# Gate and up of a decoder layer: seven block products of 256 tokens in place of eight

## The chip, the cores and the metric

The kernel runs on 1 core of one Trainium2 chip. The metric is device time in microseconds (us), from one launch of the whole layer. Five engines of the core work side by side, each through its own instruction stream: TensorE (PE, with its weight loads as PEld), VectorE (DVE), ScalarE (ACT), GpSimd (POOL) and SyncE (SP), which here only issues DMAs. They are ordered by semaphores: an instruction waits until a counter has reached a value, and a finished one raises it.

## The reference

One decoder layer over 512 tokens of width 1024, in float32:

```
h = x
h = h + 0.5 * swiglu(rmsnorm(h), ffn1_w_gate, ffn1_w_up, ffn1_w_down)
u = rmsnorm(h);  proj = u @ w_in
merged = gate_pool * pool_branch(proj) + gate_attn * window_attention(proj)
h = h + merged @ w_out
h = h + 0.5 * swiglu(rmsnorm(h), ffn2_w_gate, ffn2_w_up, ffn2_w_down)

swiglu(x, w_gate, w_up, w_down) = (silu(x @ w_gate) * (x @ w_up)) @ w_down
```

The hidden width of both feed-forward networks (FFN) is 2816, 22 tiles of 128 (f-tiles). The change is in the products x @ w_gate and x @ w_up of both.

## The kernel before

Activations lie transposed: the 128 partitions hold channels, the free dimension holds the 512 tokens, and the 1024 channels are eight tiles (k-tiles). All weights come as one stream of 182 *units* of 512 KB, each 128 partitions by eight tiles of 128 columns. For gate and up, a unit is one f-tile: eight k-tiles of stationary weights. Units pass through four slots (`raw`, `high`, `low`).

Every product is made in three matmuls of a reduced float32 format (fp32r). A number is split into a high part, which that format holds, and a low part, what is left: `wh·xh + wh·xl + wl·xh` (`passes`, lines 320 to 327). So a unit is 24 matmuls of 128x128 by 512 columns. The high part of a unit is a copy on ScalarE (`refill`, line 604) that waits until TensorE has used the slot's last unit. The low part is a subtraction on GpSimd (`low_part`, line 858). SyncE loads the next unit into `raw` when the low part has been made (line 306).

`ffn_up` on TensorE (line 361) goes through the 22 f-tiles: gate unit, up unit, in PSUM banks 4 to 7 in turn. VectorE (`ffn_up`, line 961) scales both by `rinv`, the factor of the rmsnorm, which isn't ready until after the first products: `norm_factor` (line 952) is made while TensorE works on the first four units, and the fifth unit must wait until tile 0 has been scaled out of its bank. ScalarE makes the tanh (silu is made from it) and the high part of the hidden tile, VectorE its low part. Then `ffn_down` (line 390) multiplies the hidden tiles with 22 units of `w_down`. Queues of all engines are in order: an instruction that waits holds back all behind it on its engine.

Between the two FFNs come the projections, the pooling branch, the attention (lines 439 to 579) and the output projections. The change leaves their order as it is.

## Time and profile before

| | |
|---|---|
| Time, median of 3 runs | 1095.8 us (1095.75 to 1096.73) |
| Span of the profiled execution, first to last instruction | 1090.5 us |
| Time outside that span, against the median | 5.3 us |
| PE busy | 1073.4 us, 4872 matmuls |
| PEld busy | 874.1 us, 4872 |
| DVE busy | 507.5 us, 746 |
| ACT busy | 413.0 us, 623 |
| POOL busy | 475.4 us, 208 |
| HBM read | 98.17 MB, 92 GB/s over the span |

The page of the profile lists no time of the profiled execution beside its span; its own time is taken as the median, 5.3 us over the span. Busy shares are averages over the whole span. PE's matmuls overlap in the records (each is listed some 0.39 us long, but they start every 0.23 us), so its pace is read from starts. In the first part of FFN1 (gate and up, 34.6 to 265 us) PE was busy in 230.3 of 230.4 us, DVE in 120.2, ACT in 84.6 and POOL in 108.1.

### The profile page before, as it was taken

What the parts mean: (1) busy time and instruction counts of PE and PEld (TensorE: products, weight loads), DVE (VectorE), ACT (ScalarE), POOL (GpSimd) and SP (SyncE); (2) the same over time, 40 slices, a digit from 0 to 9 for tenths busy, and PEclk for the clock granted to TensorE, in tenths of its full rate; (3) what the DMA queues carried; (4) which work ended last, traced back from release to release, by engine and by line L of the source; (5) the groups of instructions that cost most, each with busy time, mean ns of one, the idle gap of its engine ahead of it and who ended that gap; (6) DMA issues with size and microseconds to landing.
All of it is one profiled execution on the core that took longest, in us unless ns stands there. A gap on an engine that the chain in (4) does not pass through costs nothing.

```text
span 1090.5 us, 13935 instructions
## 1 busy us (share of the span) xinstructions
PE 1073.4 (98%) x4872; PEld 874.1 (80%) x4872; DVE 507.5 (47%) x746; ACT 413.0 (38%) x623; POOL 475.4 (44%) x208
## 2 busy tenths in 40 slices
PE   7999999999999999999999999999999999999998
PEld 5788888888888887887777788888888888888887
DVE  6854454543030386326766656676454545430101
ACT  6334333332131324247676643343333333421110
POOL 1553444444444424345545444444444444444440
PEclk9999999999999999999999999999999999999999
DMA  6333333323223222221111122323222322333331
GB/s 229 113 115 96 96 96 96 96 87 107 96 81 112 78 87 97 78 93 63 58 58 58 59 78 97 97 78 105 93 95 92 97 95 96 96 97 96 97 97 38
DMA packets 28684, 100.67 MB, mean 92 GB/s; under 512 B 3312, under 2 KB 3312, under 8 KB 28656
## 3 DMA queue, kind: packets, MB, share of 16 engines
q1 hardware_dynamic: 28512, 100.02, 28.2%
q8 instruction: 19, 0.31, 0.1%
q10 hardware_dynamic: 144, 0.26, 0.1%
q14 instruction: 9, 0.07, 0.0%
HBM read 98.17 MB, written 2.10 MB: 92 GB/s over the span
## 4 chain that ended last, share of the span: by engine, by line
PE 91%; DVE 6%; issue 1%; ACT 1%; DMA 1%; SPq 0%; DVEq 0%; ACTq 0%
PE psum L325 29%; PE psum L327 29%; PE psum L326 28%; DVE window_sums L1060 1%; PE psum L513 1%; PE psum L528 1%; PE psum L541 1%; PE psum L542 1%; PE psum L543 1%; DVE rinv L957 1%; PE psum L434 1%; DMA h<-x_dram 1%; DVE probs L1136 1%; DVE probsT_low L1172 0%; DVE score_max L1141 0%
## 5 line engine op out<-in xcount | busy, mean ns | idle before, releaser
L861 POOL TENSOR_TENSOR w_low<-w_raw,w_high 128x1024 fp32r<-128x1024 f32 x180 | 439.1, 2441 | 521.7 <-ACT w_high L610 521.7
L325 PE MATMUL psum<-u_high,w_high 128*128 128x512 f32 x944 | 375.5, 398 | 9.2 <-DVE w_low L1019 7.5
L327 PE MATMUL psum<-u_high,w_low 128*128 128x512 f32 x944 | 371.7, 394 | 0.0
L326 PE MATMUL psum<-u_low,w_high 128*128 128x512 f32 x944 | 369.3, 391 | 0.0
L610 ACT ACTIVATE w_high<-w_raw 128x1024 fp32r<-128x1024 f32 x180 | 190.3, 1058 | 333.0 <-PE psum L327 332.8
L325 PEld LDWEIGHTS psum<-u_high,w_high 128*128 128x128 f32 x944 | 177.8, 188 | 49.8 <-DVE w_low L1019 7.5
L326 PEld LDWEIGHTS psum<-u_low,w_high 128*128 128x128 f32 x944 | 177.9, 188 | 39.8 <-issue 1.0
L327 PEld LDWEIGHTS psum<-u_high,w_low 128*128 128x128 f32 x944 | 177.7, 188 | 38.8
L327 PE MATMUL psum<-hid_high,w_low 128*128 (+1 forms) x352 | 138.3, 393 | 0.0
L325 PE MATMUL psum<-hid_high,w_high 128*128 (+1 forms) x352 | 137.6, 391 | 0.0
L326 PE MATMUL psum<-hid_low,w_high 128*128 (+1 forms) x352 | 137.3, 390 | 0.0
L978 DVE TENSOR_TENSOR up<-up,gate 128x512 f32<-128x512 f32 x44 | 118.1, 2685 | 1.5
L943 DVE SCALAR_TENSOR_TENSOR h<-psum,h 128x512 f32<-128x512 f32 x24 | 16.6, 692 | 216.4 <-PE psum L327 216.3
L971 DVE TENSOR_TENSOR up<-psum,rinv 128x512 f32<-128x512 f32 x44 | 30.4, 691 | 179.0 <-PE psum L327 179.0
L645 ACT ACTIVATE hid_high<-up 128x512 f32 x44 | 27.8, 632 | 136.8 <-DVE up L978 136.8
L326 PEld LDWEIGHTS psum<-hid_low,w_high 128*128 128x128 f32 x352 | 66.1, 188 | 15.1
L327 PEld LDWEIGHTS psum<-hid_high,w_low 128*128 128x128 f32 x352 | 66.1, 188 | 14.3
L325 PEld LDWEIGHTS psum<-hid_high,w_high 128*128 128x128 f32 x352 | 66.1, 188 | 14.0
L883 POOL TENSOR_TENSOR probs<-probs,inv_denominator 128x1024 f32<-128x1024 f32 x16 | 30.3, 1896 | 71.6 <-DVE inv_denominator L1154 71.6
L980 DVE TENSOR_TENSOR hid_low<-up,hid_high 128x512 f32 x44 | 32.9, 747 | 40.2 <-ACT hid_high L645 40.2
L777 ACT ACTIVATE probs<-probs,neg_max,rq_now 128x256 f32<-128x256 f32 x64 | 37.6, 595 | 2.5 <-DVE sink_minus_max L1147 2.1
L932 DVE SCALAR_TENSOR_TENSOR u_low<-h,params,u_high 128x512 fp32r<-128x512 f32 x24 | 30.7, 1295 | 14.1 <-ACT u_high L622 13.9
(146 smaller groups left out, 932.3 us busy)
## 6 DMA issues: line engine op xcount, KB each, us to landing
w_raw<-weights_dram SPq DMA_DIRECT2D x181, 512.0 KB, 3.3
out_dram<-h SPq DMA_DIRECT2D x8, 256.0 KB, 3.2
h<-x_dram SPq DMA_DIRECT2D x3, 512.0 KB, 6.7
h<-x_dram SPq DMA_DIRECT2D x2, 256.0 KB, 4.2
w_raw<-weights_dram SPq DMA_DIRECT2D x2, 256.0 KB, 4.4
consts<-consts_dram SPq DMA_DIRECT2D x1, 352.0 KB, 9.1
poolw_raw<-poolw_dram ACTq DMA_DIRECT2D x1, 256.0 KB, 3.5
params<-params_dram SPq DMA_DIRECT2D x1, 31.0 KB, 1.8
```

Source lines behind the costliest of these rows:

```text
L325: pe.matmul(o, wh, xh, start=start, stop=False)
L326: pe.matmul(o, wh, xl, start=False, stop=False)
L327: return pe.matmul(o, wl, xh, start=False, stop=stop)
L610: act.activation(high[:, s, :], raw[:, s, :], ACT.Copy).then_inc(high_done, 1)
L645: act.activation(F["hid_h"][:, bass.ds(f, 1), :], F["up"][:, k:k + 1, :], ACT.Copy).then_inc(F["hidden_high"], 1)
L777: act.activation(prob[:, j % 2, a, :], prob[:, j % 2, a, :], ACT.Exp, bias=nmax[:, j % 2, a:a + 1], scale=rqn[:, 4 * j + a:4 * j + a + 1], ...
L861: pool.tensor_tensor(low[:, s, :], raw[:, s, :], high[:, s, :], ALU.subtract).then_inc(low_done, 1)
L883: pool.tensor_tensor(p, p, rden[:, j % 2, :].unsqueeze(2).to_broadcast([P, 4, 2 * BLK]), ALU.mult).then_inc(probs_ready, 1)
L932: dve.scalar_tensor_tensor(out=tile(lo, c), in0=tile(h, c), scalar=at(gains[n], c), in1=tile(hi, c), op0=ALU.mult, op1=ALU.subtract).then_ ...
L971: dve.tensor_tensor(v, psum[:, 5 + 2 * k, :], rinv[:, :], ALU.mult).then_inc(F["up_scaled"], 1)
L978: dve.tensor_tensor(v, v, g, ALU.mult).then_inc(F["hidden"], 1)
L980: dve.tensor_tensor(tile(F["hid_l"], f), v, tile(F["hid_h"], f), ALU.subtract).then_inc(F["hidden_low"], 1)
```

## The change

The products of gate and up run over *pairs* of f-tiles in all but the first tiles of each FFN: 6 plain f-tiles and 8 pairs in FFN1, 4 plain and 9 pairs in FFN2 (`PLAIN`, `PAIRS`). A pair's weights are 2 x 2 blocks (two f-tiles by two halves of the k-tiles), the normed activations 2 x 2 blocks as well (halves of the k-tiles by halves of the tokens, 256 each). Four blocks times four blocks would be eight block products; the kernel makes seven out of sums of blocks (the scheme of Strassen and Winograd). A block product is 4 k-tiles x 3 passes = 12 matmuls of 256 columns; gate and up together are 14 products a pair, at positions 0 to 13 in this order: a11 gate, a12 gate, a11 up, a12 up, s2 gate, s1 gate, s2 up, s1 up, s3 gate, s4 gate, s3 up, s4 up, a22 gate, a22 up.

- Weights of a pair, for gate and for up: `a1` (two blocks) and `s31` (two blocks) are loaded, 512 KB each, and `a22` a second time, 256 KB. GpSimd makes two sums in place in `s31` (`sum_blocks`), VectorE two more, `s2` and `s4` (`weight_sums`). ScalarE makes the high parts of all, VectorE the low parts of `a1`, `s2`, `s31`, GpSimd those of `s4` and `a22` (`late_lows`). Low parts overwrite the full values.
- Activations, once an FFN: `scale_blocks` makes the normed input (now times `rinv` beforehand, 8 instructions of 512 elements a partition), `sum_blocks` on VectorE four sums of 1024, ScalarE seven high parts of 1024, `moving_lows` seven low parts of 1024.
- Results of a pair: since the products are shared among outputs, ScalarE copies six partial results of 256 tokens out of PSUM (`copy_part`) and VectorE adds six others to them (`add_part`). `second_tile` finishes the pair's second f-tile (four instructions of 256 tokens) at the start of the next pair in VectorE's stream.
- High and low parts of the hidden tiles are made late, in the last pair and beside the down products, since their memory is that of the activation blocks.
- In the plain and down units the low part overwrites `raw`, so SyncE loads a unit when TensorE has used the slot (`load_used`) and no longer when its low part is made. All loops of the FFNs are written out. Every tensor has a fixed address.

The core of the diff; comments and blank lines are left out.

```diff
+PLAIN = (6, 4)
+PAIRS = tuple((FT - p) // 2 for p in PLAIN)
+STEPS = 14
...
+            def load_used(u):
+                sp.wait_ge(unit_used, u - SLOTS + 1)
+                load(u)
+            def pairs(n):
+                for i in range(PAIRS[n]):
+                    if i + 1 < PAIRS[n]:
+                        sp.wait_ge(product, done(n, i, 1))
+                        load_a1(n, i + 1, 0, gate_w)
+                        sp.wait_ge(product, done(n, i, 3))
+                        load_a1(n, i + 1, 1, up_w)
+                    if i + 2 < PAIRS[n]:
+                        sp.wait_ge(product, done(n, i, 8))
+                        load_s31(n, i + 2, 0, gate_w)
+                        sp.wait_ge(product, done(n, i, 10))
+                        load_s31(n, i + 2, 1, up_w)
+                    if i + 1 < PAIRS[n]:
+                        sp.wait_ge(product, done(n, i, 12))
+                        load_a22(n, i + 1, 0, gate_w)
+                        sp.wait_ge(product, done(n, i, 13))
+                        load_a22(n, i + 1, 1, up_w)
...
+            def multiply(bank, wh, wl, xh, xl, fresh):
+                o = psum[:, bank, 0:HT]
+                for c in range(HALF):
+                    w = slice(c * P, (c + 1) * P)
+                    pe.matmul(o, wh[:, w], xh[:, c, :], start=fresh and c == 0, stop=False, skip_group_check=not fresh)
+                    pe.matmul(o, wh[:, w], xl[:, c, :], start=False, stop=False, skip_group_check=not fresh)
+                    mm = pe.matmul(o, wl[:, w], xh[:, c, :], start=False, stop=c == HALF - 1,
+                                   skip_group_check=not fresh)
+                mm.then_inc(product, 1)
...
+            def pair(n, i, F):
...
+                def a11(k, w):
+                    pe.wait_ge(w["low"], 3 * g + 1)
+                    if i >= 2:
+                        pe.wait_ge(pair_hidden if k else pair_silu, 3 * g - 3)
+                    else:
+                        pe.wait_ge(F["up_scaled" if k else "gate_scaled"], PLAIN[n] - 1)
+                    moving(1)
+                    multiply(x + k, w["a_h"][:, one], w["a_l"][:, one], ub_h[:, B11], ub_l[:, B11], True)
...
+                def s2(k, w):
+                    pe.wait_ge(w["low"], 3 * g + 2)
+                    pe.wait_ge(part_copied, 6 * g + 1 + k)
+                    moving(3)
+                    multiply(x + k, w["s2_h"], w["s2_l"], ts_h[:, NT2], ts_l[:, NT2], False)
...
+                def a22(k, w):
+                    pe.wait_ge(w["late"], 2 * g + 2)
+                    pe.wait_ge(part_summed, 6 * g + 3 + 2 * k)
+                    moving(7)
+                    multiply(x + k, w["a22_h"], w["a22_l"], ts_h[:, T4], ts_l[:, T4], False)
+                for k, w in enumerate((gate_w, up_w)):
+                    a11(k, w)
+                    a12(k, w)
+                for k, w in enumerate((gate_w, up_w)):
+                    s2(k, w)
+                    s1(k, w)
+                for k, w in enumerate((gate_w, up_w)):
+                    s3(k, w)
+                    s4(k, w)
+                a22(0, gate_w)
+                a22(1, up_w)
...
+            def plain(n, base, F):
+                p = PLAIN[n]
+                g = first_pair(n)
+                for f in range(p - 4):
+                    plain_tile(n, base, f, F)
+                for b in (B11, B21, B22):
+                    block_high(n, b)
+                plain_tile(n, base, p - 4, F)
+                for t, count in ((NT2, 2), (NT1, 2), (T3, 3), (T4, 4)):
+                    sum_high(n, t, count)
+                plain_tile(n, base, p - 3, F)
+                high_a1(g, gate_w)
+                high_s2(g, gate_w)
+                high_s31(g, gate_w)
+                plain_tile(n, base, p - 2, F)
+                high_a1(g, up_w)
+                high_s2(g, up_w)
+                high_s31(g, up_w)
+                plain_tile(n, base, p - 1, F)
+            def pair(n, i, base, F):
+                g = first_pair(n) + i
...
+                more = i + 1 < PAIRS[n]
...
+                act.wait_ge(product, done(n, i, 0))
+                if i:
+                    act.wait_ge(pair_hidden, 3 * g - 2)
+                else:
+                    act.wait_ge(F["hidden"], PLAIN[n])
+                copy_part(gate_t[:, 0, left], x)
+                if i:
+                    act.wait_ge(product, done(n, i - 1, 12))
+                high_late(g, gate_w)
+                act.wait_ge(product, done(n, i, 2))
+                copy_part(up[:, 0, left], x + 1)
+                if i:
+                    act.wait_ge(product, done(n, i - 1, 13))
+                else:
+                    act.wait_ge(unit_used, base + 2 * PLAIN[n])
+                high_late(g, up_w)
+                act.wait_ge(product, done(n, i, 4))
+                copy_part(gate_t[:, 0, right], x)
+                act.wait_ge(product, done(n, i, 5))
+                if i:
+                    act.wait_ge(pair_hidden, 3 * g)
+                copy_part(gate_t[:, 1, right], 6)
+                if more:
+                    high_a1(g + 1, gate_w)
+                act.wait_ge(product, done(n, i, 6))
+                copy_part(up[:, 0, right], x + 1)
+                act.wait_ge(product, done(n, i, 7))
+                copy_part(up[:, 1, right], 7)
+                if more:
+                    high_a1(g + 1, up_w)
+                    high_s2(g + 1, gate_w)
+                    act.wait_ge(product, done(n, i, 8))
+                    high_s31(g + 1, gate_w)
+                else:
+                    refill(base + 2 * PLAIN[n], 0, U_DN1 // SLOTS + 1 if not n else U_DN2 // SLOTS + 1, first=True)
+                    for f in range(4):
+                        hidden_high(n, f, F)
+                act.wait_ge(part_summed, 6 * g + 4)
+                if i:
+                    act.wait_ge(pair_silu, 3 * g)
+                act.activation(th[:, 0, :], gate_t[:, 0, :], ACT.Tanh, scale=0.5).then_inc(pair_tanh, 1)
+                if more:
+                    high_s2(g + 1, up_w)
+                    act.wait_ge(product, done(n, i, 10))
+                    high_s31(g + 1, up_w)
+                else:
+                    hidden_high(n, 4, F)
+                    hidden_high(n, 5, F)
+                act.activation(th[:, 1, right], gate_t[:, 1, right], ACT.Tanh, scale=-0.5).then_inc(pair_tanh, 1)
+                act.wait_ge(product, done(n, i, 12))
+                act.activation(th[:, 1, left], psum[:, x, left], ACT.Tanh, scale=-0.5).then_inc(pair_tanh, 1)
...
+            def sum_blocks(g, w):
+                s31, one, two = w["s31"][g % 2], slice(0, UNIT // 2), slice(UNIT // 2, UNIT)
+                pool.wait_ge(w["s31_landed"][g % 2], 16 * (g // 2 + 1))
+                pool.tensor_tensor(s31[:, two], s31[:, two], s31[:, one], ALU.add)
+                pool.wait_ge(w["a_landed"], 16 * (g + 1))
+                pool.tensor_tensor(s31[:, one], s31[:, one], w["a"][:, one], ALU.add).then_inc(w["s31_summed"][g % 2], 1)
+            def late_lows(g, w):
+                pool.wait_ge(w["high"], 5 * g + 4)
+                pool.tensor_tensor(w["s4_l"][g % 2][:, :], w["s4"][g % 2][:, :], w["s4_h"][:, :],
+                                   ALU.subtract).then_inc(w["late"], 1)
+                pool.wait_ge(w["high"], 5 * g + 5)
+                pool.tensor_tensor(w["a22_l"][:, :], w["a22"][:, :], w["a22_h"][:, :],
+                                   ALU.subtract).then_inc(w["late"], 1)
+            def ffn(n, base, first):
+                for u in range(base + first, base + 2 * PLAIN[n]):
+                    low_part(u, u % SLOTS, raw_low)
+                    if u == base + 4:
+                        sum_blocks(first_pair(n), gate_w)
+                sum_blocks(first_pair(n), up_w)
+                for i in range(PAIRS[n]):
+                    g = first_pair(n) + i
+                    late_lows(g, gate_w)
+                    if i + 1 < PAIRS[n]:
+                        sum_blocks(g + 1, gate_w)
+                    late_lows(g, up_w)
+                    if i + 1 < PAIRS[n]:
+                        sum_blocks(g + 1, up_w)
+                b = base + 2 * PLAIN[n]
+                for u in range(b, b + 2 * DOWN):
+                    low_part(u, u % SLOTS, raw_low)
...
+            def scale_blocks(n):
+                for c in range(DT):
+                    kh, kt = c // HALF, c % HALF
+                    dve.scalar_tensor_tensor(
+                        out=ub[:, 2 - 2 * kh:4 - 2 * kh, kt, :], in0=h[:, c, :].rearrange("p (a t) -> p a t", a=2),
+                        scalar=at(gains[2 * n], c), in1=rinv[:, :].rearrange("p (a t) -> p a t", a=2),
+                        op0=ALU.mult, op1=ALU.mult).then_inc(u_scaled, 1)
+            def sum_blocks(n):
+                dve.wait_ge(u_scaled, DT * (n + 1))
+                dve.tensor_tensor(ts[:, NT1], ub[:, B11], ub[:, B12], ALU.subtract).then_inc(ts_summed, 1)
...
+            def moving_lows(n):
+                for lo, full, hi, count in (
+                        (ub_l[:, B11], ub[:, B11], ub_h[:, B11], 1), (ub_l[:, B21], ub[:, B21], ub_h[:, B21], 2),
...
+            def weight_sums(g, w):
+                dve.wait_ge(w["a_landed"], 16 * (g + 1))
+                dve.wait_ge(w["s31_summed"][g % 2], g // 2 + 1)
+                s1 = w["s31"][g % 2][:, UNIT // 2:UNIT]
+                dve.tensor_tensor(w["s2"][:, :], s1, w["a"][:, 0:UNIT // 2], ALU.add).then_inc(w["summed"], 1)
+                dve.wait_ge(w["summed"], 2 * g + 1)
+                dve.tensor_tensor(w["s4"][g % 2][:, :], w["s2"][:, :], w["a"][:, UNIT // 2:UNIT], ALU.add
+                                  ).then_inc(w["summed"], 1)
...
+            def plain(n, base, F):
+                p = PLAIN[n]
+                g = first_pair(n)
+                for f in range(p - 4):
+                    plain_tile(n, base, f, F)
+                scale_blocks(n)
+                plain_tile(n, base, p - 4, F)
+                sum_blocks(n)
+                plain_tile(n, base, p - 3, F)
+                moving_lows(n)
+                weight_sums(g, gate_w)
+                plain_tile(n, base, p - 2, F)
+                low_a1(g, gate_w)
+                low_s2(g, gate_w)
+                low_s31(g, gate_w)
+                dve.wait_ge(unit_used, base + 2 * p - 1)
+                weight_sums(g, up_w)
+                low_a1(g, up_w)
+                plain_tile(n, base, p - 1, F)
+                low_s2(g, up_w)
+                low_s31(g, up_w)
...
+            def pair(n, i, F):
+                g = first_pair(n) + i
+                x = 4 * ((i + PAIRS[n]) % 2)
+                f = PLAIN[n] + 2 * i
+                more = i + 1 < PAIRS[n]
+                def add_part(to, bank, pos, copied):
+                    dve.wait_ge(product, done(n, i, pos))
+                    dve.wait_ge(part_copied, 6 * g + copied)
+                    dve.tensor_tensor(to, psum[:, bank, left], to, ALU.add).then_inc(part_summed, 1)
+                if i:
+                    second_tile(n, i - 1)
+                add_part(gate_t[:, 0, left], 2, 1, 1)
+                add_part(up[:, 0, left], 3, 3, 2)
+                if more:
+                    dve.wait_ge(product, done(n, i, 4))
+                    weight_sums(g + 1, gate_w)
+                    low_a1(g + 1, gate_w)
+                    dve.wait_ge(product, done(n, i, 6))
+                    weight_sums(g + 1, up_w)
+                    low_a1(g + 1, up_w)
+                    low_s2(g + 1, gate_w)
+                add_part(gate_t[:, 1, right], x, 8, 4)
+                if more:
+                    low_s31(g + 1, gate_w)
+                else:
+                    hidden_low(0, F)
+                    hidden_low(1, F)
+                add_part(gate_t[:, 0, right], 6, 9, 3)
+                add_part(up[:, 1, right], x + 1, 10, 6)
+                add_part(up[:, 0, right], 7, 11, 5)
+                if more:
+                    low_s2(g + 1, up_w)
+                    low_s31(g + 1, up_w)
+                dve.wait_ge(pair_tanh, 3 * g + 1)
+                dve.scalar_tensor_tensor(out=gate_t[:, 0, :], in0=th[:, 0, :], scalar=1.0, in1=gate_t[:, 0, :],
+                                         op0=ALU.add, op1=ALU.mult).then_inc(pair_silu, 1)
+                dve.wait_ge(pair_silu, 3 * g + 1)
+                dve.wait_ge(part_summed, 6 * g + 6)
+                dve.tensor_tensor(hid[:, f, :], gate_t[:, 0, :], up[:, 0, :], ALU.mult).then_inc(pair_hidden, 1)
```

## Rows read from the trace of the kernel before

**Rows 1.** The page: span and busy us of each engine.

```profile
span 1090.5 us, 13935 instructions
...
PE 1073.4 (98%) x4872; PEld 874.1 (80%) x4872; DVE 507.5 (47%) x746; ACT 413.0 (38%) x623; POOL 475.4 (44%) x208
```

**Rows 2.** PE in order of time inside FFN1: start, duration, line; 24 matmuls of 512 columns apart.

```profile
100.01 0.39 PE L325 MATMUL psum<-u_high,w_high 128*128 128x512 f32 x1
...
105.50 0.39 PE L325 MATMUL psum<-u_high,w_high 128*128 128x512 f32 x1
```

**Rows 3.** The same view in the attention: 256 columns, two row halves at once, four steps apart.

```profile
490.68 0.28 PE L513 MATMUL psum<-k_block_low,q_block_high 64*128 64x256 f32 x2
...
491.16 0.28 PE L513 MATMUL psum<-k_block_high,q_block_low 64*128 64x256 f32 x2
```

**Rows 4.** The same view: eight matmuls of two columns, each with a weight load.

```profile
465.18 0.95 PE L434 MATMUL psum<-consts,q_squares 128*128 128x2 f32 x8
```

**Rows 5.** DVE and POOL in order of time in FFN1.

```profile
102.04 2.42 POOL L861 TENSOR_TENSOR w_low<-w_raw,w_high 128x1024 fp32r<-128x1024 f32 x1 [3.09 <-ACT w_high L610]
...
102.22 2.78 DVE L978 TENSOR_TENSOR up<-up,gate 128x512 f32<-128x512 f32 x1
```

**Rows 6.** DVE and POOL in order of time, both with several instructions queued.

```profile
410.39 5.23 POOL L861 TENSOR_TENSOR w_low<-w_raw,w_high 128x1024 fp32r<-128x1024 f32 x2 [4.82 <-ACT w_high L610]
...
410.85 2.50 DVE L1060 TENSOR_TENSOR window_sums<-pool_in 128x512 f32<-128x512 f32 x1
413.38 4.23 DVE L1060 TENSOR_TENSOR window_sums<-window_sums 128x512 f32<-128x512 f32 x3
```

**Rows 7.** Groups by line: busy us, mean ns of one, idle before, releaser.

```profile
L610 ACT ACTIVATE w_high<-w_raw 128x1024 fp32r<-128x1024 f32 x180 | 190.3, 1058 | 333.0 <-PE psum L327 332.8
...
L799 ACT ACTIVATE attn_high<-psum 64x256 fp32r<-64x256 f32 x8 | 3.0, 373 | 3.2 <-PE psum L543 3.1
...
L877 POOL TENSOR_TENSOR v_block_low<-v_tokens,v_block_high 128x256 fp32r<-128x256 f32 x4 | 2.9, 729 | 0.0
```

**Rows 8.** DVE in order of time, and the POOL instruction beside its last two.

```profile
519.97 1.28 DVE L1114 SCALAR_TENSOR_TENSOR q_block_low<-q,params,q_block_high 128x1024 fp32r<-128x1024 f32 x1
...
420.06 0.68 DVE L1047 TENSOR_TENSOR k_raw<-psum,rinv 128x512 f32<-128x512 f32 x1
420.67 0.68 DVE L1047 TENSOR_TENSOR v_raw<-psum,rinv 128x512 f32<-128x512 f32 x1
...
420.45 2.36 POOL L861 TENSOR_TENSOR w_low<-w_raw,w_high 128x1024 fp32r<-128x1024 f32 x1 [4.84 <-ACT w_high L610]
```

**Rows 9.** Start of FFN1: POOL, PE and DVE in order of time.

```profile
28.71 2.42 POOL L861 TENSOR_TENSOR w_low<-w_raw,w_high 128x1024 fp32r<-128x1024 f32 x1 [2.73 <-ACT w_high L610]
...
34.66 0.49 PE L325 MATMUL psum<-u_high,w_high 128*128 128x512 f32 x1 [1.54 <-DVE gate L968]
...
78.92 0.69 DVE L971 TENSOR_TENSOR up<-psum,rinv 128x512 f32<-128x512 f32 x1 [4.67 <-PE psum L327]
```

**Rows 10.** Start of FFN2: DVE and ACT in order of time.

```profile
735.08 1.99 DVE L948 TENSOR_TENSOR sum_of_squares<-rinv 128x512 f32<-128x512 f32 x1
...
738.30 0.69 DVE L959 TENSOR_TENSOR rinv<-rinv,sum_of_squares 128x512 f32<-128x512 f32 x1
...
746.80 0.69 DVE L971 TENSOR_TENSOR up<-psum,rinv 128x512 f32<-128x512 f32 x1 [1.34 <-PE psum L327]
...
768.77 0.69 DVE L971 TENSOR_TENSOR up<-psum,rinv 128x512 f32<-128x512 f32 x1 [4.68 <-PE psum L327]
...
732.98 1.06 ACT L610 ACTIVATE w_high<-w_raw 128x1024 fp32r<-128x1024 f32 x1
```

**Rows 11.** PE in order of time in the first matmuls of the kernel.

```profile
8.50 0.63 PE L327 MATMUL psum<-u_high,w_low 128*128 128x512 f32 x1
8.93 0.63 PE L325 MATMUL psum<-u_high,w_high 128*128 128x512 f32 x1
```

**Rows 12.** DMA issues of the page: KB each, median us from issue to landing.

```profile
w_raw<-weights_dram SPq DMA_DIRECT2D x181, 512.0 KB, 3.3
```

614 lines of the change are left out of this document (413 added, 201 removed).

## The prediction

> **What bounds the kernel now.** I read the page first. The reader is to see that TensorE is busy in 98% of the span [rows 1]; so the end moves with its work and its waits. In order of time its starts inside FFN1 are evenly spaced: 24 matmuls of 512 columns, one unit, take 105.50 - 100.01 = 5.49 us, 0.229 us each [rows 2]. The other engines have room, but VectorE and GpSimd don't use theirs independently. At 102.04 GpSimd starts a subtraction of 2.42 us, at 102.22 VectorE a product of two tensors in SBUF, which ends at 105.00: GpSimd's end plus the 0.55 that it needs itself [rows 5]. With both queues full they take turns: GpSimd's two take 5.23 instead of 4.8 (one VectorE instruction lies between them), and VectorE's take 2.5 instead of 0.6 each time they meet one [rows 6]. So every instruction of VectorE with two SBUF inputs and every one of GpSimd share one resource, and its time adds up. An instruction with one input in PSUM isn't held: two of them start 0.61 apart, 0.68 long, over a GpSimd subtraction that runs from 420.45 [rows 8].
>
> **What is removed: matmul time.** Before, two f-tiles are four units, 4 x 5.49 = 21.96 us. A pair is 14 products x 12 = 168 matmuls of 256 columns. The trace has no such matmul over 128 rows. The nearest are those of the attention: 256 columns in two row halves start every (491.16 - 490.68) / 4 = 0.120 us [rows 3]. Bounds: half of a 512-column one, 0.1145 [rows 2]; and with a weight load that doesn't hide well, 0.127: eight weight loads with two columns each behind them need about 0.11 apiece (0.95 less some 0.2 of the last one's length, over seven) [rows 4], and 0.229 - 0.1145 leaves 0.015 a matmul for what doesn't shrink. I take 0.120: a product 1.44 us, a pair 20.2 us (19.2 to 21.3). If nothing else waited, 17 pairs would give back 17 x 1.8 = 31 us (11 to 47).
> The Trainium skill (TensorE: Matmul & The Clock Gate, "Wait — 56ns, not 53.3ns?") has 2.4 GHz matmuls start every N/2.4 + 2.5 ns, 109 ns at 256 columns; the trace disagrees at 512 (229 against 216). By it a pair would be 18.3 us; it would only matter where TensorE sets the pace.
>
> **What is added, by duration.** VectorE with two SBUF inputs: 512 elements hold it 0.60 (start to start 0.61 [rows 8]), 1024 about 1.15 (1.28 long, next one earlier [rows 8]), 256 about 0.35. GpSimd: 1024 elements 2.42 [rows 5], 256 0.73 [rows 7], so 512 by the line between them 1.29, 1.24 back to back (bounds 1.2 and 1.3). ScalarE: 1024 1.06, 256 0.37 [rows 7], 512 about 0.6. A handover from TensorE costs 0.2, others 0.1 (102.04 + 2.42 to VectorE's next).
>
> **A pair in the steady state.** The shared resource: GpSimd 8 x 1.24 = 9.9; VectorE weight sums 4 x 0.6, lows of a1 and s31 4 x 1.15, of s2 2 x 0.6, silu and product of the first tile 1.2, of the second 0.7, in all 10.1. Together 20.0 us of a 20.2 us pair, before any wait for order. In order, with M the time in the pair at which VectorE has finished the previous pair's first tile (the copy of the first product into that buffer waits for it):
> - ScalarE copies and makes the high part of s4: M + 1.15. GpSimd makes its two gate lows and the two gate sums of the next pair, 4 x 1.24: Z = M + 6.1. The a1 load waits for position 1 (3.1) and lands 3.3 later [rows 12], 6.4: not late.
> - From Z VectorE's first weight sum may start, but GpSimd's next is queued and goes first, as in [rows 6]. They alternate: four of GpSimd (4.8), two weight sums and the a1 low of VectorE (2.3): Z + 7.1. Only now are the up sums there: two weight sums, two lows, 2.95, and the add of position 8, 0.35: Z + 10.4. TensorE's position 12 waits for this add. At Z = 9 that is 19.4, against 17.3 at TensorE's pace: a stall of 2.1 us.
> - Behind it stand the s31 low and two adds; the second releases position 13 at Z + 12.35, which ends at P = Z + 13.8.
> - ScalarE's tanh waits for an add (Z + 11.9), and two highs behind it hold back VectorE's last low to Z + 14.3; with silu and product VectorE is through at Z + 16.7 = P + 2.9. So M = 2.9, Z = 9.0 and P = 22.8 us.
> The bounds are 20.3 (turns fall out well, TensorE sets the pace) and 23.8 (some more handovers). I take 22.8, since each step is a row or lies in order: 0.8 a pair *slower* than four units. The last pair of each FFN has no weight sums and runs at TensorE's 20.2. 13 steady pairs: +10.9 (range -21 to +24); 2 last: -3.6.
>
> **Start of the pairs in FFN2.** Baseline: VectorE sees unit 3 end at 746.80 and unit 7, the last plain one, at 768.77 [rows 10]. `rinv` comes at 737.7, 1.3 earlier than now (738.30 + 0.69, less the 1.3 that the instruction at 735.08 waited for GpSimd): no GpSimd instruction falls on it, since the high of unit 4, now made at 732.98 [rows 10], stands in ScalarE's queue behind three highs that wait for `scale_blocks`.
> - scale_blocks 8 x 0.6: 742.8. Three highs and unit 4's: 746.9; its low 749.4. TensorE wanted it at 746.6: stall 2.8.
> - Then GpSimd makes the two gate sums before unit 5's low, taking turns with the silu of tile 0 and VectorE's sums: 756.3, stall 1.5. Unit 6's high stands behind the highs of the sums, which wait for VectorE: low at 764.9, stall 3.0. Unit 7 ends at 775.9, 7.3 late.
> - VectorE: tile 1 until 768.3; seven moving lows 7.9 with two GpSimd sums between, 778.6; weight sums 779.8; tile 2 with tanh 782.9; the gate a1 low 784.1. Position 0 waits for it: 8.2 more. Position 2 waits for the up a1 low, 788.2: 1.15 more. The pair is 17.0 late.
> - In this pair GpSimd's lows start at 792.0 (tile 3's product, then copy and high), 6.4 in the pair where the steady state has 4.1; the same chain gives a22 4.9 late, a pair of 25.5: 3.5 over four units.
> **In FFN1** two tiles stand before `scale_blocks`, but GpSimd's two gate sums now follow unit 4's low (28.71 to 31.1 [rows 9]) and fall on the steps of `rinv`: 2.1 later, and TensorE already waits there, at 34.66 after 1.54 of idle [rows 9]. Then unit 10's low 1.9 late, and by the same list VectorE's gate a1 low at 90.9 instead of 78.7 (unit 11's end [rows 9]), the up one 4.1 later: 13.7 late. First pair +3.5.
> Bound of both from below: without turns VectorE's list in FFN2 (27 us of its own from 737.7, some 6 of waits for tanh) ends at 771, 2 late; half of each chain seems the least, 20 together; from above 48. I take 17.0 + 13.7 + 7.0 = 37.7.
>
> **What stays.** The down products: loads of units now wait for TensorE (3.3 + 1.06 + 2.42 = 6.8 and handovers [rows 5, 7, 12], needed 16.5 later), hidden lows 0.6 each against two a unit of 5.49: hidden. 256 KB more per matrix and pair, some 130 GB/s: hidden. Attention and projections: unchanged. Unrolled code removes table loads of ScalarE, which had idle time: 0.
>
> **Sum.** 37.7 + 10.9 - 3.6 = +45 us on a profiled execution of 1090.5 span [rows 1] and 5.3 outside, which is the median 1095.8: 1141 us.
>
> **Rivals.**
> 1. *TensorE sets the pace in the pairs* (turns fall better than in my list: VectorE's ops get in ahead of GpSimd's queued ones). P = 20.3 in 13 pairs: -21.6 instead of +10.9: 1095.8 + 37.7 - 21.6 - 3.6 = 1108. For it: 20.0 us of shared work fit in 20.2. Against: [rows 6] shows the queued GpSimd instruction goes on first.
> 2. *The other side, faster:* the turns exist but the block work before the pairs is covered. Its place is the stretch from `rinv` to position 0, its price 20 us in place of 37.7; it decides for faster once the pairs run at 20.3 too and the two starts cost less than 25: 1095.8 + 20 - 21.6 - 3.6 = 1091. For it: by VectorE's own durations the list is only 2 us late. Against: every meeting in [rows 5, 6].
> 3. *The clock falls in the stalls.* The kernel's first matmuls start every 0.43 us, 1.2 GHz, for 4.6 us [rows 11], after idle time. The stalls of 8 us ahead of position 0 may bring this back, 2.3 us each by these rows; most of it lies under VectorE's lateness. 1141 to 1146. The Trainium skill (the same page, "HAM oscillation") says that gaps of TensorE re-throttle it; no stretch inside this trace shows it.
> 4. *The 256-column matmuls don't hide their weight load* (0.106 + 0.11 = 0.22): a pair of 36 us: 1095.8 + 17 x 14 = over 1330. Against: [rows 3] have a load in every step.
>
> **Chances.** Forecast 0.55 (own range 1125 to 1158), rival 1 and what lies between 0.22, rival 2 0.12, clock 0.06, loads 0.02, no visible change (gains and starts cancel) 0.03. Range 1100 to 1158, which leaves out rival 2 and the loads. A measurement of this kernel tells 0.2% (2.2 us) from no change. Faster 0.12, within 0.03, slower 0.85.
>
> **What would show it.** Start to start of the 256-column matmuls 0.120; a pair's period on TensorE 22.8 with idle ahead of positions 12 and 13, put down to VectorE's adds; idle before position 0 of 8 us in each FFN, put down to the a1 low; unit 4 of FFN2 waiting for its low; GpSimd's and VectorE's SBUF instructions nowhere overlapping. Wrong if TensorE shows no idle in the pairs, or if position 0 starts within 3 us of the last plain unit.

## The result, and the profile after

| | before | after |
|---|---|---|
| Time, median of 4 runs each | 1095.9 us (1095.75 to 1096.73) | 1144.9 us (1142.59 to 1146.99) |
| Ratio | | 1.0446 [1.0430, 1.0463] |
| Span of the profiled execution | 1090.5 us | 1142.9 us |

The change makes the kernel 49 us slower; 1141 was forecast. The page of the changed kernel answers to [rows 1]: TensorE is busy for less time, in a longer span. The row of its clock has eights where the pairs begin in FFN1, and in the plain tiles and the first pair of FFN2, and the chain that ended last runs 18% on VectorE and 14% on GpSimd.

```profile
span 1142.9 us, 15754 instructions
...
PE 1064.4 (93%) x6096; PEld 927.1 (81%) x6096; DVE 699.8 (61%) x1022; ACT 482.1 (42%) x838; POOL 517.5 (45%) x276
...
PEclk9998999999999999999999999998889999999999
...
PE 57%; DVE 18%; POOL 14%; issue 5%; ACT 4%; DMA 2%; DVEq 0%; SPq 0%; ACTq 0%
```

The two profiled executions lie 52.4 us apart, the medians 49.0. The profile of the kernel before is of an execution at full clock (1.000). Of its 48 executions beside the later runs, 8 have that clock: they take 1091.9 to 1093.0 us, and each span is 1.8 us shorter than its time. So that profile stands for about 1092.3 us and not for the median, and the time outside the span is 1.8 us in both kernels (1144.8 for a span of 1142.9). The 5.3 us of the table ahead of the prediction are these 1.8 and 3.5 of clock.

The waits of PE in the changed kernel, longest sum first (us in all, times, longest). Line 1505 is `add_part`, the wait of 13 steady pairs ahead of position 12. Line 1432 is the low part of a1 ahead of position 0. The "issue" waits are those ahead of position 12 in the two first pairs (5.13 and 4.78). They are waits for the same add: in FFN1 position 12 starts at 115.03, and VectorE's add for it ran from 114.51 to 114.93. L1241 is the low part of a plain unit.

```profile
PE psum L529 <- DVE gate L1505: 25.9, 13, 2.3
PE psum L529 <- DVE gate_a_low L1432: 13.6, 2, 7.6
PE psum L529 <- issue: 9.9, 2, 5.1
PE psum L476 <- POOL w_low_in_place L1241: 7.2, 3, 3.0
PE psum L476 <- DVE w_low_in_place L1584: 6.8, 1, 6.8
```

**Where the 52.4 us of span went.** All are differences of starts on PE. Position 0 comes at 90.52 in FFN1, where unit 12 came at 78.72: +11.8. In FFN2 it comes 59.62 after the first product of the FFN, for 44.82: +14.8. The two first pairs take 28.95 and 29.36 for 21.97, four units: +14.4. The 13 steady pairs take 23.0 on the mean: +13.4. The last two take 20.4 and 20.2: -3.4. The stretch from the end of gate and up in FFN1 to FFN2 is 2.6 longer: 4.3 more at the norm and the first projections, less what the down and output products save. The last down products are 1.2 shorter. The sum is 52.4.

Start of FFN1's pairs on PE in the changed kernel (start, duration, idle before and releaser in brackets). The reader is to see the idle before position 0, then matmuls 0.21 apart until 94.53 and 0.12 after it, and the same again from 115.03, which is position 12 of the first pair.

```profile
82.56 0.39 PE L478 MATMUL psum<-ffn_u_high,w_low_in_place 128*128 128x512 f32 x1
90.52 0.58 PE L529 MATMUL psum<-u_blocks_high,gate_a_high 128*128 128x256 f32 x1 [7.58 <-DVE gate_a_low L1432]
...
94.32 0.41 PE L531 MATMUL psum<-u_blocks_high,gate_a_low 128*128 128x256 f32 x1
94.53 0.32 PE L529 MATMUL psum<-u_blocks_high,gate_a_high 128*128 128x256 f32 x1
94.81 0.28 PE L531 MATMUL psum<-u_blocks_high,gate_a_low 128*128 128x256 f32 x1
...
115.03 0.51 PE L529 MATMUL psum<-moving_sums_high,gate_a_high 128*128 128x256 f32 x1 [5.13 <-issue]
...
118.32 0.36 PE L529 MATMUL psum<-moving_sums_high,up_a_high 128*128 128x256 f32 x1
118.52 0.28 PE L530 MATMUL psum<-moving_sums_low,up_a_high 128*128 128x256 f32 x1
```

The same by stretches (start and end, length, busy us and count of PE, PEld, DVE, ACT and POOL, granted clock, DMA share, GB/s): the first pair of FFN1, the six after it, the first pair of FFN2. The granted clock is 0.87 and 0.80 in the first pairs and 0.98 in the six between.

```profile
90.52:119.47 28.95, 23.82 (x169) 23.63 (x169) 21.95 (x27) 12.52 (x22) 12.45 (x8) 0.87 0.24 77
119.47:257.98 138.51, 126.10 (x1010) 124.19 (x1009) 99.91 (x133) 62.49 (x114) 71.73 (x48) 0.98 0.33 108
...
809.84:839.20 29.36, 24.58 (x168) 24.40 (x169) 22.37 (x28) 12.52 (x22) 12.45 (x8) 0.80 0.24 81
```

**A steady pair**, the fourth of FFN1, position 0 at 164.43. GpSimd, VectorE and the wait of PE that ends last. GpSimd's first four run from 168.26 to 173.29. Then VectorE's two sums and a low, 0.69 and 1.22 long when alone, take 1.67, 1.67 and 2.14, because GpSimd's next instruction goes first each time. VectorE is free for the up sums at 180.32, and the add that TensorE waits for starts at 183.59, after two lows.

```profile
168.26 1.30 POOL L1253 TENSOR_TENSOR gate_s_low<-gate_s,gate_s_high 128x512 fp32r<-128x512 f32 x1 [11.08 <-ACT gate_s_high L906]
...
173.26 1.29 POOL L1253 TENSOR_TENSOR up_s_low<-up_s,up_s_high 128x512 fp32r<-128x512 f32 x1
174.51 1.74 POOL L1256 TENSOR_TENSOR up_a_low<-up_a,up_a_high 128x512 fp32r<-128x512 f32 x1
...
177.91 2.28 POOL L1249 TENSOR_TENSOR up_s<-up_s,up_a 128x512 f32<-128x512 f32 x1
...
173.43 1.67 DVE L1424 TENSOR_TENSOR gate_s<-gate_s,gate_a 128x512 f32<-128x512 f32 x1 [2.61 <-POOL gate_s L1249]
...
176.90 2.14 DVE L1432 TENSOR_TENSOR gate_a_low<-gate_a,gate_a_high 128x1024 fp32r<-128x1024 f32 x1
180.32 0.69 DVE L1424 TENSOR_TENSOR up_s<-up_s,up_a 128x512 f32<-128x512 f32 x1 [1.28 <-POOL up_s L1249]
...
183.59 0.42 DVE L1505 TENSOR_TENSOR gate<-psum,gate 128x256 f32<-128x256 f32 x1
...
184.15 0.36 PE L529 MATMUL psum<-moving_sums_high,gate_a_high 128*128 128x256 f32 x1 [2.28 <-DVE gate L1505]
```

### The profile page after: what moved, and what is told of

Its sections match the earlier page's. It is cut to its first block, busy times and chain, and to the rows that moved or that the text cites. A ratio compares the mean times of both kernels' runs of the same rounds, so it can differ in the third digit from the quotient of the medians.

```text
span 1142.9 us, 15754 instructions
## 1 busy us (share of the span) xinstructions
PE 1064.4 (93%) x6096; PEld 927.1 (81%) x6096; DVE 699.8 (61%) x1022; ACT 482.1 (42%) x838; POOL 517.5 (45%) x276
## 4 chain that ended last, share of the span: by engine, by line
PE 57%; DVE 18%; POOL 14%; issue 5%; ACT 4%; DMA 2%; DVEq 0%; SPq 0%; ACTq 0%
PE psum L476 14%; PE psum L478 13%; PE psum L477 13%; PE psum L529 4%; PE psum L530 4%; PE psum L531 4%; POOL up_s L1249 3%; POOL up_s L1247 2%; POOL up_a_low L1256 2%; POOL gate_s L1249 2%; POOL up_s_low L1253 2%; POOL gate_s_low L1253 1%; DVE window_sums L1625 1%; POOL gate_a_low L1256 1%; POOL gate_s L1247 1%
## 5 line engine op out<-in xcount | busy, mean ns | idle before, releaser
L1241 POOL TENSOR_TENSOR w_low_in_place<-w_raw,w_high 128x1024 fp32r<-128x1024 f32 x62 | 153.8, 2485 | 210.8 <-ACT w_high L848 210.7
L848 ACT ACTIVATE w_high<-w_raw 128x1024 fp32r<-128x1024 f32 x112 | 117.9, 1054 | 191.9 <-DMA w_raw<-weights_dram 150.2
L1241 POOL TENSOR_TENSOR w_low<-w_raw,w_high 128x1024 fp32r<-128x1024 f32 x50 | 122.8, 2456 | 117.6 <-ACT w_high L848 117.6
L477 PE MATMUL psum<-hidden_low,w_high 128*128 128x512 f32 x352 | 137.0, 389 | 0.0
L476 PE MATMUL psum<-hidden_high,w_high 128*128 128x512 f32 x352 | 137.0, 389 | 0.0
L478 PE MATMUL psum<-hidden_high,w_low_in_place 128*128 128x512 f32 x352 | 137.0, 389 | 0.0
L476 PE MATMUL psum<-u_high,w_high 128*128 128x512 f32 x240 | 98.9, 412 | 0.4 <-DVE u_low L1341 0.3
L477 PE MATMUL psum<-u_low,w_high 128*128 128x512 f32 x240 | 94.1, 392 | 0.0
L478 PE MATMUL psum<-u_high,w_low 128*128 128x512 f32 x240 | 94.0, 392 | 0.0
L476 PE MATMUL psum<-ffn_u_high,w_high 128*128 128x512 f32 x160 | 66.7, 417 | 17.3 <-POOL w_low_in_place L1241 7.2
L477 PEld LDWEIGHTS psum<-hidden_low,w_high 128*128 128x128 f32 x352 | 66.1, 188 | 13.7
```

The source lines that it names most:

```text
L476: pe.matmul(o, wh, xh, start=start, stop=False)
L477: pe.matmul(o, wh, xl, start=False, stop=False)
L478: return pe.matmul(o, wl, xh, start=False, stop=stop)
L848: act.activation(high[:, s, :], raw[:, s, :], ACT.Copy).then_inc(high_done, 1)
L1241: pool.tensor_tensor(wlow[:, s, :], raw[:, s, :], high[:, s, :], ALU.subtract).then_inc(low_done, 1)
```

## The experiments

Theory 1 is the prediction's: GpSimd and VectorE take turns, and the order of the queues makes the turns late for TensorE. Experiments e1 to e5 and e8 test it, and its rival in each is named in the expectation. Experiments e6, e7, e9 and e10 are about something found in the traces and not foreseen.

### e1: GpSimd's pair work without reading SBUF

Each of the eight instructions becomes two fills; each fill waits for the one before it. The sums s3 and s1 and the low parts of s4 and a22 are thus not computed.

```diff
 def sum_blocks(g, w):
-    pool.tensor_tensor(s31[:, two], s31[:, two], s31[:, one], ALU.add)
+    fill(s31[:, two])
+    fill(s31[:, two])
...
```

> Each of the eight GpSimd instructions of a pair (two sums in s31, the lows of s4 and a22, for gate and up) is replaced by two fills with zero of the same 512 elements, with the same waits; so the weight sums and those lows are not computed. GpSimd then reads nothing from SBUF but keeps its place in the order. Theory 1 (GpSimd and VectorE take turns at SBUF): VectorE's two-input instructions are no longer held, means fall to 0.69 us (512 elements) and 1.22 (1024) in the pairs, and a steady pair falls from 23.0 to 20.3-20.8 us; the run to 1080-1105 us. Theory 2 (the pair is bound by the order of the queues and by GpSimd's own chain, not by turns): if the two fills last as long as one sum (some 1.2-1.3 us), the steady pair stays within 0.5 of 23.0. The trace shows how long a fill is; if it is far shorter, the run tells only an upper bound.

Measured: 1089.0 us, span 1087.0, in a single run, so there is no interval. VectorE's two groups of the gate sums and the low of a1, first as the changed kernel has them, then as e1 has them (count, busy us, mean ns):

```profile
L1432 DVE TENSOR_TENSOR gate_a_low<-gate_a,gate_a_high 128x1024 fp32r<-128x1024 f32 x17 | 34.5, 2029 | 1.6
L1424 DVE TENSOR_TENSOR gate_s<-gate_s,gate_a 128x512 f32<-128x512 f32 x17 | 26.4, 1554 | 38.9 <-POOL gate_s L1249 38.9
```

```profile
L1442 DVE TENSOR_TENSOR gate_a_low<-gate_a,gate_a_high 128x1024 fp32r<-128x1024 f32 x17 | 20.8, 1224 | 9.8 <-ACT gate_a_high L895 9.6
L1434 DVE TENSOR_TENSOR gate_s<-gate_s,gate_a 128x512 f32<-128x512 f32 x17 | 11.8, 691 | 27.9 <-POOL gate_s L1259 24.7 <-PE psum L532 3.2
```

Every pair but the first of each FFN takes 20.16 us, 14 x 1.44, with no wait. GpSimd still has work in every place (two fills take about 1.1 us, one instruction before 1.3), and VectorE now runs beside it. The shorter fills alone don't explain it: they bring VectorE's first sum from 9.0 to 7.9 us in the pair, and the add that TensorE waits for now ends 1.4 us before it is needed. So without the turns the written order is not late. The first pairs are 24.0, so the turns account for 5 of the 7 us there. Theory 1 is shown for the steady pair. The Trainium skill (SBUF — State Buffer, "SBUF: two separate sides") says that a VectorE instruction with two SBUF inputs locks out GpSimd only where that one reads SBUF; the rows agree on both halves, 1554 against 691 ns.

### e2: the late high parts ahead of the copy on ScalarE

```diff
+if i: act.wait_ge(product, done(n, i - 1, 12))
+high_late(g, gate_w)
 act.wait_ge(product, done(n, i, 0))
 ...
 copy_part(gate_t[:, 0, left], x)
-if i: act.wait_ge(product, done(n, i - 1, 12))
-high_late(g, gate_w)
```

> One move on ScalarE in every pair: the high parts of gate's s4 and a22 stand ahead of the copy of the first product, which waits for VectorE's last product of the pair before. Theory 1 (the cycle VectorE's end M -> copy -> highs -> GpSimd -> weight sums sets the steady pair): GpSimd starts with the pair, the first weight sum comes at 7.9 instead of 9.0 in the pair (then the landing of a1 is next), a steady pair 21.7 us instead of 23.0, a first pair 24-25 instead of 29, the whole 1145 - 13 x 1.3 - 2 x 4.5 = 1119 us (1110-1127). Theory 2 (the shared SBUF work alone sets the pair, order is indifferent): within 3 us of 1145.

Measured: 1131.9 us (1130.68 to 1133.12), ratio 1.0335 [1.0309, 1.0360]. The steady pairs fall from 23.0 to 22.1, where 21.7 was expected: GpSimd starts earlier, and the turns then come earlier. The first pairs stay at 28.2 and 29.2, where 24 to 25 was expected. Position 12 still starts at 23.9 in them, for 24.5. ScalarE comes to these instructions only after the tanh of the last plain tile, which waits for VectorE. GpSimd then starts 6.2 us into FFN1's first pair for 8.1, but its first four instructions take 6.9 for 5.6, in turns with VectorE's last plain product and the up lows. So VectorE's first sum comes at 13.3 for 13.9. The total of 1119 was missed by 13, most of it there. Theory 2 (within 3 us of 1145) is refuted.

### e3: VectorE's adds in the order in which TensorE wants them

On top of e2. The add of position 8 goes ahead of the up sums, that of 10 ahead of the low of s31, that of 11 behind it.

```diff
     low_a1(g + 1, gate_w)
-    dve.wait_ge(product, done(n, i, 6))
-    weight_sums(g + 1, up_w); low_a1(g + 1, up_w); low_s2(g + 1, gate_w)
 add_part(gate_t[:, 1, right], x, 8, 4)
 if more:
-    low_s31(g + 1, gate_w)
+    weight_sums(g + 1, up_w); low_a1(g + 1, up_w)
 add_part(gate_t[:, 0, right], 6, 9, 3)
 add_part(up[:, 1, right], x + 1, 10, 6)
+if more:
+    low_s2(g + 1, gate_w); low_s31(g + 1, gate_w)
 add_part(up[:, 0, right], 7, 11, 5)
```

> As the run with the highs first, and VectorE takes the add of position 8 before the up weight sums and those of 9 and 10 before the lows of gate's s2 and s31. Theory 1: positions 12 and 13 no longer wait, TensorE's stalls in the steady pairs go to under 0.5 us, a steady pair 20.3-21.0 us, the whole 1102 us (1095-1112). Theory 2 (20 us of turns in a pair of 20.2 can't be packed): the steady pair stays at 21.5 or more, the stall moves from position 12 to positions 0-4 of the next pair or to the a1 lows, and the whole stays within 4 us of the run with the highs first.

Measured: 1106.7 us (1106.46 to 1107.82), ratio 1.0107 [1.0083, 1.0130]. Position 12 now follows position 11 without a wait; what is left of the waits of PE is this (view as above):

```profile
PE psum L529 <- DVE gate_a_low L1430: 15.1, 2, 7.6
...
PE psum L529 <- issue: 5.4, 4, 1.8
PE psum L529 <- ACT gate L911: 2.8, 11, 0.3
```

The steady pairs take 20.4 to 20.8, and 21.6 the one behind FFN2's first. The 0.4 over TensorE's own 20.16 is position 4's wait for a copy on ScalarE. The same work, still in turns, is 2.4 us a pair cheaper in another order than as changed. So the loss takes both: the turns (e1) and an add that TensorE waits for queued late behind them.

### e4: the high parts of the plain units ahead of those of the blocks

Alone, on the changed kernel. ScalarE makes the highs of units 4 to 7 (in FFN1 8 to 11) two at a time ahead of the three and of the four block highs.

```diff
+units_of(base, p - 4)
 for b in (B11, B21, B22):
     block_high(n, b)
-plain_tile(n, base, p - 4, F)
+plain_tile(n, base, p - 4, F, False)
+units_of(base, p - 3)
 ...
```

> Only the start of the pairs: ScalarE makes the high parts of the next plain units before those of the activation blocks and of their sums. Theory 1 (VectorE's list of block work, in turns with GpSimd, sets position 0): the stalls of units 4 to 7 of FFN2 and of unit 10 of FFN1 go (9 and 2 us), but position 0 comes at most 2 us earlier in each FFN; the whole 1145 - 0 to 4 us. Theory 2 (the order of the highs on ScalarE sets the start): position 0 comes 7-9 us earlier in FFN2 and 2 in FFN1; the whole about 1135 us.

Measured: 1138.0 us (1136.78 to 1140.27), ratio 1.0386 [1.0361, 1.0410]. Position 0 comes 1.6 earlier in FFN1 and 2.4 earlier in FFN2: the stalls of the plain units of FFN2 stay, now as waits for VectorE (2.46 and 4.15). These are 4.0 of the 4.5 us between the two profiled spans; the medians are 7 apart, and the other 2.4 are in no trace. In FFN2 positions 0 and 1 now take 4.39 for 5.15, since the clock falls later there, and yet position 12 comes 24.49 after position 0 in both kernels; the section on the prediction comes back to it. Theory 1 allowed 2 us of start in each FFN and 4 in all, theory 2 7 to 9 in FFN2: the first has the place right, but the time came out past its bound.

### e5: the three orders together

> The changed kernel with all three orders of the earlier experiments at once: the four unit highs ahead of the block highs and ScalarE's late block highs ahead of its other late work, and VectorE's additions for the sums made early in the pair. Theory 1 (the steady pair is set by the turns of GpSimd and VectorE, and the first pair by ScalarE's order and the clock) adds the effects: the pair-level orders gave 1106.7, and the unit order took 2.4 us off the second start, left pair 8's products at nearly full clock and was worth 7 us on the changed kernel; some of that is the same clock time that the other orders give back, so 1100 us, between 1097 and 1104. Rival (the first pair is late for its sums only, which the unit order does not touch): 1104 to 1107.

Measured: 1103.8 us (1102.93 to 1105.31), ratio 1.0079 [1.0060, 1.0098]. This is the upper end of what was expected and the lower end of the rival's, so the total does not decide between them. The starts do: position 0 comes at 87.77 for e3's 88.62, and 57.03 after the start of FFN2 for 59.66, while the first pairs stay at 25.5 and 25.2 for 26.1 and 25.2.

### e8: six plain f-tiles in FFN2 as well

```diff
-PLAIN = (6, 4)
+PLAIN = (6, 6)
```

On e5: one pair less in FFN2, two plain f-tiles more. The expectation describes this edit wrongly (six for eight, and one pair more).

> The experiment with all orders (e5), with six plain units for eight ahead of the pairs and so one more pair in each FFN, if its number of tiles allows it. Theory 1: with a steady pair of 20.5 us for two units of 10.9 (21.9 for two positions of the before) each further pair for two plain units takes 1.4 us off, and the pair that comes first is put where the norm of the second half still runs: 2 to 4 us less than e5, 1096 us (1092 to 1102). Rival (the pair-level lists need the plain units as cover: their blocks are not ready when the pair begins, and TensorE waits for them): 1102 to 1112, slower than e5.

Measured: 1096.6 us (1094.84 to 1097.34), ratio 1.0008 [0.9997, 1.0019]; 7.2 less than e5. The number that was expected came, by the opposite of the reason given for it. The pair's 20.6 us become four units of 5.44, 21.8, so 1.1 is lost there. But position 0 now comes 70.39 after the start of FFN2, and without the four further units that is 48.6 for 57.03. The stalls of the plain units of FFN2 are gone, and a gap of 4.1 ahead of its position 0 is left:

```profile
PE psum L529 <- DVE gate_a_low L1436: 4.1, 1, 4.1
PE psum L529 <- issue: 2.9, 2, 1.8
```

So what FFN2 lacked was plain work for TensorE beside the block work. More than six isn't possible in this layout, since the seventh hidden tile lies on the normed input that plain tiles still read; it wasn't tried.

### e6, e7, e9, e10: where the operands lie

The changed kernel's 512-column matmuls start every 0.2268 us and not every 0.2289, also in the down products. There 24 of them, one unit, take 5.44 where [rows 2] have 5.49:

```profile
300.13 0.39 PE L476 MATMUL psum<-hidden_high,w_high 128*128 128x512 f32 x1
...
305.57 0.39 PE L476 MATMUL psum<-hidden_high,w_high 128*128 128x512 f32 x1
```

Every tensor has another address there. The four experiments leave the kernel before as it is and only add unused memory: 64 bytes ahead of the weight buffers (e6), the same and 64 behind them (e7), 192 behind them (e9), 128 behind them (e10).

```diff
 low = sb("w_low", [P, SLOTS, UNIT], F32R)
+pad_b = sb("pad_b", [P, 48])
 consts = sb("consts", [P, CONSTS])
```

> The kernel before with 64 bytes of unused memory ahead of its weight buffers, nothing else: every buffer moves up 64 bytes, so that weight tiles begin at 64 and activation tiles at 0 modulo 128 bytes in a partition, where in the kernel before it is the other way round. The 512-column product runs at 0.2289 us a matmul in the kernel before and 0.2268 in the changed one, also in the attention part that the change leaves alone. Theory A (the moving operand's address sets it; in the changed kernel both kinds of tile begin at 64): the rhs here is at the other phase than in both, so the pitch is anything between; if the stationary side or the sum of both counts, it stays 0.2289 and the time 1095.8; if weights at 64 are what is fast, 0.2268 and 1087, from some 4,370 matmuls by 2.1 ns. Theory B (the placement has no part in it, the mix of the program has): 0.2289 and 1095.8.

> The kernel before with 64 unused bytes ahead of the weight buffers and 64 more ahead of the constants, so that weight and activation tiles both begin at 64 modulo 128 bytes, as in the changed kernel; the instructions are the same. Theory A (the placement of operands sets the pitch of 512-column matmuls): pitch 0.2268 for 0.2289, 4,370 matmuls by 2.1 ns, 9 us less: 1087 us (1085 to 1089), less than both kernels. Theory B (placement has no part): 1095.8 and 0.2289.

> The kernel before with 192 unused bytes between the weight buffers and the constants, nothing else. Byte addresses in a partition: let d be the address of the activation tiles less that of the weight tiles, modulo 256. The kernel before and e6 have d = 64 and both showed 0.2289 us a 512-column matmul; e7 has d = 128 and showed 0.2324; the changed kernel has d = 0 and shows 0.2268. Here d = 0 (all of them 128 modulo 256). Theory A (the distance between the two operands modulo 256 sets the pitch): 0.2268, 4,370 matmuls by 2.1 ns, 9 us less: 1087 us (1085 to 1089). Theory B (a distance modulo 2048 counts: it is 1280 here, 0 in the changed kernel): between, or no change, 1090 to 1096. Theory C (the pitch is the program's, its mix of shapes): 0.2289 and 1095.8.

> The kernel before with 128 unused bytes between the weight buffers and the constants: the distance d of activation tiles from weight tiles modulo 256 is 192, the one of the four multiples of 64 that no run has. So far 0 gives 0.2268 us a 512-column matmul, 64 0.2289 and 128 0.2324. Theory A (d modulo 256 sets the pitch, and counts alike in both directions): as 64, 0.2289 and 1095.8 us (1093 to 1098). Rival (it grows with d up to the next multiple of 256): above 0.2324, over 1106.

Measured, with d the byte address of the activation tiles less that of the weight tiles, modulo 256 (all of them are the same in each kernel):

| kernel | weights mod 256 | d | pitch, us | time, us | ratio |
|---|---|---|---|---|---|
| after | 192 | 0 | 0.2268 | | |
| e9 | 128 | 0 | 0.2267 | 1087.7 (1086.43 to 1089.18) | 0.9938 [0.9919, 0.9956] |
| before | 128 | 64 | 0.2289 | 1095.8 | 1 |
| e6 | 192 | 64 | 0.2289 | 1095.8 (1092.64 to 1096.81) | 1.0000 [0.9989, 1.0012] |
| e7 | 192 | 128 | 0.2324 | 1105.5 (1104.74 to 1108.73) | 1.0094 [1.0076, 1.0111] |
| e10 | 128 | 192 | 0.2333 | 1112.7 (1112.64 to 1112.84) | 1.0149 [1.0132, 1.0166] |

One unit, 24 matmuls apart, in e9, e7 and e10, as in [rows 2]: 5.44, 5.57 and 5.60 us.

```profile
100.36 0.39 PE L326 MATMUL psum<-u_high,w_high 128*128 128x512 f32 x1
...
105.80 0.39 PE L326 MATMUL psum<-u_high,w_high 128*128 128x512 f32 x1
```

```profile
99.94 0.39 PE L327 MATMUL psum<-u_high,w_high 128*128 128x512 f32 x1
...
105.51 0.39 PE L327 MATMUL psum<-u_high,w_high 128*128 128x512 f32 x1
```

```profile
100.07 0.39 PE L326 MATMUL psum<-u_high,w_high 128*128 128x512 f32 x1
...
105.67 0.39 PE L326 MATMUL psum<-u_high,w_high 128*128 128x512 f32 x1
```

e7 refuted the first form of the theory (both at 64 modulo 128 is fast): it was slower by 0.9%. e6 left the pitch where it was. The two together with the kernel before and the changed one suggested the distance modulo 256; e9 was expected at 1087 on that ground and came at 1087.7. e10 decided for its rival: the pitch grows with d from 0 to 192 and is not the same on both sides. Modulo 2048 the distance is 0 in the changed kernel and 1280 in e9, at the same pitch, so no longer period is needed; a version of e9 with 0 modulo 2048, by 960 unused bytes, did not fit in SBUF and has no result. The size agrees roughly: 4,368 matmuls by 2.1 ns are 9 us, and 8.1 were measured; for e7 and e10 the same sum gives 15 and 19, and 9.7 and 16.6 were measured. Part of e7's gap is the clock: four of its six executions have 1.000, of the kernel before 3 of the 23 beside them. And between 500 and 625 us, in the attention, the pitch is 0.231 in e9 as in the kernel before. Only multiples of 64 were tried, and why the distance counts isn't known; that each kernel has both kinds of tiles at one phase throughout is from the addresses in the code.

**e9 beats both kernels** (its six times and the eleven of the kernel before beside them, 1092.12 to 1096.82, don't overlap), and is the fair standard: the changed kernel already has d = 0. Against it the scheme costs 57 us as changed and 9 us in its best order and split (e8). A steady pair of e8 is 20.6 us against 21.8. Gate and up of FFN2 come out even (240.8 us for 240.3), since the start and the first pair cost what the other pairs save. In FFN1 their end is 6.3 later than in e9 (259.66 for 253.35), with an idle of 7.3 us ahead of its position 0.

## Why the prediction was right

**The steady pair** was the step that mattered, and it held in size and mechanism. Forecast were 22.8 us, an add released at Z + 10.4, and a stall of 2.1. Six of the 13 take 23.02 to 23.04, three take 24.2 with a fall of the clock in them, and four take 21.9 to 22.2, each right behind a pair in which the clock fell; the mean is 23.0. In the pair above Z is 173.29 and the add starts at Z + 10.3, and position 12 is 2.4 late in most. The list of turns, instruction by instruction, gave this from [rows 5, 6, 8]. It has small slips: four GpSimd instructions at its own 1.24 are 5.0 and not 4.8, and VectorE's take a little more than its 0.6, 1.15 and 0.35. It also counted every GpSimd instruction among the turns; the fills of e1 take no part in them. The product was forecast at 1.44 from [rows 3] and is 1.44; the working of the bound 0.127 (0.229 - 0.1145 leaves 0.1145 and not 0.015) doesn't come out, but nothing hung on it. That rules out rival 4, and e1 and e3 show that rival 1's 20.3 is what another order of the same work gives (20.6), though not the order that was written.

**The starts** were forecast 17.0 and 13.7 late, and position 0 is 14.8 and 11.8 late. That is not 2 us too much in the lists: the forecast's start terms hold position 2's wait for the up low as well, and position 0 itself stands in them 15.6 and 12.2 late (784.1 and 90.9 for the gate a1 low, against 768.6 and 78.7). In FFN2 the list can be held against the trace step by step (the trace less 26.5 us, by which the changed kernel starts FFN2 later):

| end of | forecast | trace |
|---|---|---|
| `scale_blocks` | 742.8 | 743.1 |
| low part of unit 4 | 749.4 | 749.4 |
| low part of unit 5 | 756.3 | 756.1 |
| low part of unit 6 | 764.9 | 764.5 |
| seven moving lows | 778.6 | 778.0 |
| tile 2 | 782.9 | 782.2 |
| gate a1 low | 784.1 | 783.3 |
| up a1 low | 788.2 | 787.7 |
| GpSimd's first low of the pair starts | 792.0 | 791.5 |

```profile
776.03 0.47 PE L476 MATMUL psum<-ffn_u_high,w_high 128*128 128x512 f32 x1 [2.99 <-POOL w_low_in_place L1241]
791.15 0.77 PE L476 MATMUL psum<-ffn_u_high,w_high 128*128 128x512 f32 x1 [2.33 <-POOL w_low_in_place L1241]
809.84 0.58 PE L529 MATMUL psum<-u_blocks_high,gate_a_high 128*128 128x256 f32 x1 [6.03 <-DVE gate_a_low L1432]
...
808.57 1.22 DVE L1432 TENSOR_TENSOR gate_a_low<-gate_a,gate_a_high 128x1024 fp32r<-128x1024 f32 x1
```

Unit 4 waits 2.99 (forecast 2.8), unit 5 not at all (1.5), unit 6 2.33 (3.0), and position 0 6.03 (8.2). Rival 2 (starts covered, faster in all) is refuted by these rows. Its other half, pairs at 20.3, came nearly true in e3 and e5 (20.6), and even then 8 us were missing in e5.

**The first pairs** were forecast at 3.5 over four units each and measured at 7.0 and 7.4. More than half of the difference is the other side of the start terms: starts and first pairs together were forecast at 37.7 for both FFNs and are 41.0. Position 12 comes when the list has it, in FFN2 84.1 us after the first product of the FFN for 84.0. It waits for a chain on VectorE, ScalarE and GpSimd that begins with the last plain tile on VectorE. Product 0 had long ended, at 93.45 in FFN1, when ScalarE copied it:

```profile
97.67 0.39 ACT L911 ACTIVATE gate<-psum 128x256 f32<-128x256 f32 x1 [1.55 <-DVE hidden L1385]
98.65 1.82 POOL L1253 TENSOR_TENSOR gate_s_low<-gate_s,gate_s_high 128x512 fp32r<-128x512 f32 x1 [20.27 <-ACT gate_s_high L906]
```

**The clock** is rival 3, and the rest of the miss in this term. Behind the stalls of 7.58 and 5.13 us in FFN1 the matmuls of 256 columns start every 0.213 us for 4.0 and 3.3 us: the lower of the two levels, 1.2 GHz for 2.4. At positions 0 and 1 that costs nothing by itself, since TensorE would only have waited longer, for the up low and then for position 12. e4 shows it: there positions 0 and 1 of FFN2 are 0.8 us shorter, and position 12 starts 24.49 behind position 0 in both (829.96 - 805.47 in e4, 834.33 - 809.84 as changed).

```profile
805.47 0.39 PE L529 MATMUL psum<-u_blocks_high,gate_a_high 128*128 128x256 f32 x1 [3.74 <-DVE gate_a_low L1438]
829.96 0.55 PE L529 MATMUL psum<-moving_sums_high,gate_a_high 128*128 128x256 f32 x1 [5.11 <-issue]
```

```profile
834.33 0.55 PE L529 MATMUL psum<-moving_sums_high,gate_a_high 128*128 128x256 f32 x1 [4.78 <-issue]
```

Positions 12 and 13 take 4.4 and 4.9 with the low clock, where most steady pairs have 3.3: 1.1 and 1.6 us in the two first pairs. Three steady pairs lose 1.1 to 1.2 in the same way, behind waits of 2.3 (24.2 us for 23.0). Of these 6.2 us the next pair gives back most wherever it is a steady one: VectorE went on meanwhile, and the wait ahead of its position 12 is 1.2 to 1.5 instead of 2.3.

```profile
138.11 0.36 PE L529 MATMUL psum<-moving_sums_high,gate_a_high 128*128 128x256 f32 x1 [1.20 <-DVE gate L1505]
```

The four pairs behind such a pair are 3.8 us shorter together than 23.0 each, so the clock costs 2 to 3 us net in the pairs. The rival put it at up to 5 us, most of it under VectorE's lateness, and gave it 0.06: its size was right, but it stands beside the forecast mechanism and not in place of it. The Trainium skill (TensorE: Matmul & The Clock Gate, "HAM oscillation") says that idle gaps bring the lower clock back, and here the trace agrees.

**What was said to stay.** The last pairs (-3.6) came at -3.4, and the down products stayed hidden. Attention and projections did not stay: norm and first projections take 4.3 us more. The trace shows a place for it that the forecast had at nothing, the loads. SyncE now loads a unit only when TensorE has used the slot; ScalarE's high part waits for a landing, and `u_high` for the norm stands behind it, 2.4 us after VectorE has made its input (394.87). In the kernel before, that wait was under 0.1. The low part of the same tile then takes 2.38 instead of 0.75 on VectorE, in a turn with GpSimd.

```profile
396.30 1.06 ACT L848 ACTIVATE w_high<-w_raw 128x1024 fp32r<-128x1024 f32 x1 [4.37 <-DMA w_raw<-weights_dram]
397.26 1.32 ACT L860 ACTIVATE u_high<-h,params 128x512 fp32r<-128x512 f32 x2
```

No run tests it. About 1 us of the 4.3 lies behind that, where the clock falls at 449.6 us.

**Luck.** Against the two profiled spans the terms are: starts and first pairs 37.7 forecast and 41.0 measured, steady pairs 10.9 and 13.4, last pairs -3.6 and -3.4, all other parts 0 and 1.4. That is 45 and 52.4, and 3.5 of the difference are the clock of the kernel before. The nearly right nothing for the other parts is luck. The faster pitch, 2.1 ns in each of about 2,700 plain matmuls, is worth up to 5.7 us, for which no row of the trace before spoke; 3.0 can be seen, in the down products of both FFNs and the output products. It stands against the 4.3 us above. Without these 3.0 the time would be some 1148 us, an estimate from these numbers, and so 1141 came nearer than its terms deserve.

## What to carry to other kernels

Fewer multiplications pay only what a product of the new shape saves at its real pitch (here 21.8 to 20.2 us for a pair and not one eighth), and every sum that buys them must fit beside it on engines that may share a resource. Write the queues of those engines out instruction by instruction: the same work in another order was 38 us apart here (e3). Move first what the bottleneck engine waits for. Count a fall of its clock behind the idle only where the next step waits for this engine: here most of it lay under waits that were there anyway. And look at the addresses of matmul operands too: 192 unused bytes were worth more than the scheme.

## What the runs showed of the hardware

- The pitch of fp32r matmuls of 512 columns follows the address of the moving tiles less that of the stationary ones, modulo 256 bytes: 0.2267, 0.2289, 0.2324, 0.2333 us for 0, 64, 128, 192 (e9, before and e6, e7, e10). The 256-column ones at distance 0 start every 0.120 (after).
- A fill of GpSimd (512 elements a partition, 0.53 us) doesn't hold VectorE's two-input instructions (0.69 for a sum of 512 elements in e1), a subtraction or addition of 1.29 does (1.67 in turns, after).
- TensorE's clock fell behind idle of 7.58, 6.03, 5.13 and 4.78 us, to 1.2 GHz for some 3 to 5 us of matmuls each time, and in three steady pairs already behind 2.3; behind most waits of 2.3 it did not. Net it cost 2 to 3 us in the pairs.
